# A decoder layer on one core: bias tables by a diagonal product and a slanted store, the memory's keys and values made inside the first block

## The reference, cut to what matters

```python
def t5_bucket(rel):
    n = jnp.maximum(-rel, 0)
    max_exact = N_BUCKETS // 2
    large = max_exact + (jnp.log(jnp.maximum(n, 1).astype(jnp.float32) / max_exact)
                         / math.log(MAX_DIST / max_exact) * (N_BUCKETS - max_exact)).astype(jnp.int32)
    large = jnp.minimum(large, N_BUCKETS - 1)
    return jnp.where(n < max_exact, n, large)

# in causal_block_attention, for each block of 128 queries
rel = positions[:, None, :] - sl(positions)[:, :, None]
bias = jnp.moveaxis(rel_bias[t5_bucket(rel)], -1, 1).astype(jnp.float32)
s2 = jnp.einsum('bqhcd,bkhcd->bhcqk', sl(q_d), k_d).astype(jnp.float32) * diff_scale + bias[:, :, None]
p2 = jax.nn.softmax(jnp.where(mask, s2, NEG), axis=-1)

# in memory_cross_attention; mem_n is the normed memory, 256 rows
q = (h @ w_cq).reshape(b, s, CROSS_HEADS, CROSS_DH)
k, v = jnp.split(mem_n @ w_ckv, 2, axis=-1)
```

## Time and profile before

| | |
|---|---|
| time, median of 3 runs | 4218.0 us (4199.03 to 4221.75) |
| profiled execution, span from first to last instruction | 4102.6 us |
| median less that span (the profiled execution's own whole time is not listed) | 115.4 us |
| busy share: PE, DVE, POOL, ACT | 75%, 62%, 58%, 20% |
| mean DMA rate over the span | 325 GB/s |

### The profile page before, as it was taken

One profiled execution on the slowest core, in us unless ns is written; L12 is line 12 of the kernel. 1 busy time (PEld: TensorE's weight loads), 2 busy tenths in 40 slices (PEclk: granted clock), 3 DMA queues, 4 the chain that ended last, 5 costly groups with the idle time before them and its releaser, 6 DMA issues.

```text
span 4102.6 us, 44198 instructions
## 1 busy us (share of the span) xinstructions
PE 3080.9 (75%) x11072; PEld 1743.0 (42%) x11072; DVE 2523.6 (62%) x6096; ACT 819.6 (20%) x1925; POOL 2390.4 (58%) x2145
## 2 busy tenths in 40 slices
PE   6563789768895789768896788858897589866666
PEld 4442535434452535434452544425454354532222
DVE  8626574766649474766649465585647656476444
ACT  1110231113211231113211132112311123111111
POOL 8100576656756476556766466555565556567776
PEclk9666899879998899879998889979899799988988
DMA  4433999999998999998998899989899888998998
GB/s 142 149 98 128 350 338 399 351 327 335 390 403 308 348 330 396 357 332 325 369 394 307 334 330 376 363 315 333 307 383 343 313 321 308 401 320 318 362 366 327
DMA packets 424948, 1333.13 MB, mean 325 GB/s; under 512 B 47520, under 2 KB 48416, under 8 KB 424672
## 3 DMA queue, kind: packets, MB, share of 16 engines
q0 software_dynamic: 294912, 1073.87, 70.8%
q1 hardware_dynamic: 128608, 251.96, 17.1%
q10 hardware_dynamic: 1152, 4.19, 0.3%
HBM read 1320.46 MB, written 9.37 MB: 324 GB/s over the span
## 4 chain that ended last, share of the span: by engine, by line
PE 47%; DVE 27%; DMA 11%; issue 10%; ACT 3%; POOL 1%; DVEq 0%; POOLq 0%; ACTq 0%; SPq 0%
PE ps_sum L958 22%; PE ps_p L739 9%; PE ps_s L880 6%; DMA rows<-in_peer_v,ids_v 6%; DMA w_ring<-in_wstream 4%; DVE rows L1614 4%; DVE feat_b L1517 3%; DVE feat_b L1512 2%; PE ps_s L823 2%; PE ps_p L831 2%; DVE rows L1306 1%; DVE e L1519 1%; PE ps_s L819 1%; PE ps_t L730 1%; DVE e L1556 1%
## 5 line engine op out<-in xcount | busy, mean ns | idle before, releaser
L958 PE MATMUL ps_sum<-rows,diag 128*128 128x512 f32 x3584 | 1840.4, 650 | 517.9 <-ACT diag L1174 395.7
L546 POOL DMA_INDIRECT rows<-in_peer_u,ids_u x1024 | 1129.4, 1103 | 1171.1 <-DVE dots L1614 562.2
L555 POOL DMA_INDIRECT rows<-in_peer_v,ids_v x1024 | 1167.1, 1140 | 503.6 <-issue 281.3
L1614 DVE CUSTOM_DVE_ANT_0 rows<-rows,h_cur 128x1024 f32<-128x1024 f32 x1024 | 1223.9, 1221 | 200.7 <-DMA rows<-in_peer_u,ids_u 191.3
L958 PEld LDWEIGHTS ps_sum<-rows,diag 128*128 128x128 f32 x3584 | 699.8, 208 | 1388.0 <-issue 984.7
L739 PE MATMUL ps_p<-hT,w_ring 128*128 128x128 f32 x3968 | 520.1, 290 | 78.0 <-DVE hT L1335 56.4
L739 PEld LDWEIGHTS ps_p<-hT,w_ring 128*128 128x128 f32 x3968 | 507.2, 205 | 161.7 <-issue 78.3
L1174 ACT ACTIVATE diag<-ident,acts 128x128 f32<-128x128 f32 x896 | 316.6, 392 | 780.6 <-DVE acts L1637 399.6
L1629 DVE SCALAR_TENSOR_TENSOR x_cur<-rows,acts,x_cur 128x1024 f32<-128x1024 f32 x128 | 164.5, 1285 | 138.1 <-DMA rows<-in_peer_v,ids_v 138.1
L730 PE MATMUL ps_t<-ident,xs 128*128 128x128 f32 x192 | 42.2, 392 | 232.9 <-DVE xs L1323 175.8
L1422 DVE CUSTOM_DVE_ANT_0 e<-ps_s,bias_t 128x512 f32<-128x512 f32 (+3 forms) x96 | 82.2, 857 | 213.6 <-PE ps_s L819 102.7
(11 more groups left out here) (265 smaller groups left out, 2551.7 us busy)
## 6 DMA issues: line engine op xcount, KB each, us to landing
w_ring<-in_wstream SPq DMA_DIRECT2D x816, 256.0 KB, 7.4
bias_t<-bias_rows SPq DMA_DIRECT2D x40, 512.0 KB, 6.5
rows<-in_peer_u,ids_u POOLq DMA_INDIRECT x1024, 6.7
rows<-in_peer_v,ids_v POOLq DMA_INDIRECT x1024, 6.8
bias_rows<-rows SPq DMA_DIRECT2D x5, 960.0 KB, 4.0
bias_t<-in_x SPq DMA_DIRECT2D x8, 512.0 KB, 9.0
out<-x_cur ACTq DMA_DIRECT2D x8, 512.0 KB, 2.8
e<-in_final_gain SPq DMA_DIRECT2D x7, 512.0 KB, 7.4
```

Of the source, the lines that this page charges most:

```text
L546: pool.indirect_dma_start(u_rows[:, j % G_RING, :], None, peer_u, bass.IndirectOffsetOnAxis(ap=ids_u[:, j:j + 1], axis=0)).then_inc(u_land ...
L555: pool.indirect_dma_start(v_rows[:, j % G_RING, :], None, peer_v, bass.IndirectOffsetOnAxis(ap=ids_v[:, j:j + 1], axis=0)).then_inc(v_land ...
L958: ins = pe.matmul(ps_sum[:, c * 512:(c + 1) * 512], diag[:, n % 4, :], v_rows[:, j % G_RING, c * 512:(c + 1) * 512], start=(n == 0), stop= ...
L1614: dve.tensor_tensor_reduce(row, row, h_cur[:, :], 1.0, 0.0, ALU.mult, ALU.add, dots[:, p:p + 1]).then_inc(u_used, 1)
```

## The change

Nothing in blocks 1 to 7 is changed. In the prologue and block 0:

1. **Bias tables.** Partition p stands for the distance 127 - p. DVE compares it with 33 limits in one instruction, takes differences to get the bucket, multiplies the table with it and reduces, which gives the bias at that distance for each head, and puts it on a diagonal. PE multiplies ones by the four diagonals (128 x 128 each), which gives in each partition the same curve of 128 values. ACT copies the curves to SBUF, with the last bucket's value repeated over 896 columns ahead. POOL fills the other 1024 columns with the mask value. A band is now 128 equal rows of 2048 columns; the store gives it its slant, as the rows go to DRAM at a pitch that is one element longer than that of the loads. All five (1 MB each) are issued in a row, without a wait between them, at the start of `project_2`.
2. **Memory.** Its norm and transposes move into `project_0` and `latents` of block 0, and its 32 slices come after the 34 projection slices. PE takes one at each of the positions 24 to 55 of block 0, which lie between `gates` and `diff_3`; ACT's copies have positions too.
3. **x first.** x and the first 7 projection slices are loaded first, and DVE's `scale_x` is the first thing of size that it does.
4. The rotary arguments are made on 128 partitions with 256 columns, and stored with 8 DMAs in place of 2. The decay constants come after `latents`.

```diff
+IN_SLICES = 2 * IN_TILES
+CURVE = 2 * SEQ
+PITCH = CURVE + P
+MEM_AT = 24
...
+        bias_rows = bias_d.rearrange("h (r c) -> h r c", c=PITCH)
+        slanted = bias_d[:, 1:1 + P * (PITCH + 1)].rearrange("h (p c) -> h p c", c=PITCH + 1)
...
# SP
             sp.dma_start(cols[:, :], columns).then_inc(cols_in, 16)
+            sp.dma_start(x_in[:, :], x[0:P, :]).then_inc(x_landed, 16)
...
+            for i in range(W_RING):
+                load_w(MEM_SLICES + i, i)
             for t in range(MT):
-                sp.dma_start((e0, e1)[t][:, :], mem[t * P:(t + 1) * P, :]).then_inc(mem_in, 16)
...
+                sp.dma_start(mem_x[t][:, :], mem[t * P:(t + 1) * P, :]).then_inc(mem_in, 16)
...
+            def store_curves():
+                sp.wait_ge(pre["blank"], DIFF_H + 2)
+                sp.wait_ge(pre["curve"], DIFF_H)
+                for h in range(DIFF_H, -1, -1):
+                    sp.dma_start(slanted[h, :, 0:CURVE], curve[h]).then_inc(pre["stored"], 16)
...
+            def project_2(b):
+                if isinstance(b, int):
+                    store_curves()
+                front_loads(b, per_tile * 7, per_tile * 11)
...
+            def opening(p):
+                i = p - MEM_AT + W_RING
+                if W_RING <= i < MEM_SLICES:
+                    load_w(i, IN_SLICES + i)
+                elif MEM_SLICES <= i < MEM_SLICES + W_RING:
+                    front_loads(0, IN_SLICES + (i - MEM_SLICES), IN_SLICES + (i - MEM_SLICES) + 1)
...
# PE
+            def curves():
+                pe.wait_ge(pre["on_diag"], DIFF_H)
+                for h in range(DIFF_H):
+                    ins = pe.matmul(ps_s[:, h * P:(h + 1) * P], ones[:, :], on_diag[:, h, :], start=True, stop=True)
+                ins.then_inc(pre["curve_ps"], 1)
+
+            def turn_mem():
+                for t in range(MT):
+                    pe.wait_ge(pre["xs"], t + 1)
                     if t:
+                        pe.wait_ge(pre["curve"], DIFF_H)
+                    for k in range(KT):
+                        ins = pe.transpose((ps_sum, ps_s)[t][:, k * P:(k + 1) * P], mem_x[t][:, k * P:(k + 1) * P], ident[:, :])
                     ins.then_inc(pre["turned"], 1)
...
+            def opening(p):
+                if MEM_AT <= p < MEM_AT + MEM_SLICES:
+                    mem_piece(p - MEM_AT)
...
+            def first_project():
+                project(0, 0, 0, 3)
+                curves()
+                turn_mem()
...
# ACT
+            def out_curves():
+                act.wait_ge(pre["curve_ps"], 1)
+                for h in range(DIFF_H):
+                    copy(curve[h][:, 0:near], bc(ps_s[:, h * P:h * P + 1], [P, near]))
+                    copy(curve[h][:, near:SEQ], ps_s[:, h * P:(h + 1) * P]).then_inc(pre["curve"], 1)
...
+            def first_exps():
+                early_exps()
+                project_4(0)
...
# DVE
+                prepare(dve.tensor_scalar(reached, limits, away, None, ALU.is_le))
+                prepare(dve.tensor_tensor(inside, reached[:, 0:BUCKETS], reached[:, 1:BUCKETS + 1], ALU.subtract))
+                prepare(dve.tensor_tensor(picked.rearrange("p (k h) -> p k h", h=DIFF_H), table.rearrange("p (k h) -> p k h", h=DIFF_H),
+                                          bc(inside.unsqueeze(2), [P, BUCKETS, DIFF_H]), ALU.mult))
+                prepare(dve.tensor_reduce(by_away, picked.rearrange("p (k h) -> p h k", h=DIFF_H), AX_X, ALU.add))
+                for h in range(DIFF_H):
+                    dve.tensor_scalar(on_diag[:, h, :], ident[:, :], by_away[:, h:h + 1], None, ALU.mult).then_inc(pre["on_diag"], 1)
...
+            def first_latents():
+                buckets()
+                scale_mem()
+                positions_read()
+                gain_mem()
+                lambdas()
+                latents(0)
+                decays()
```

More of the change, by code:

```diff
@@ L415, in store_mask @@
                             sp.wait_ge(pre["band"], b * (DIFF_H + 1) + (h + 1))
[L416 to L433, removed]
+                            sp.dma_start(bias_rows[h, bass.ds(b * P + P, P), 0:SEQ], rows[:, h, :]).then_inc(pre["stored"], 16)
+                    sp.wait_ge(pre["stored"], 16 * (NB + 1) * (DIFF_H + 1))
                 sp.nop()
@@ new lines, in spread_angles, with rope_sines @@
+            def spread_angles():
+                act.wait_ge(cols_in, 16)
+                at, own = slice(COL["freq"], COL["freq"] + 2), slice(NOPE, NOPE + ROPE)
+                for a in (0, 1, 3):
+                    copy(cols[a * ROPE:(a + 1) * ROPE, at], cols[own, at]).then_inc(pre["spread"], 1)
+            def rope_sines():
+                for c, t in enumerate((cosines, sines)):
+                    act.wait_ge(pre["rope_arg"], c + 1)
+                    act.activation(t, t, ACT.Sin).then_inc(act_step, 1)
+                    act.wait_ge(act_step, c + 1)
+                    if c == 0:
+                        act.nop().then_inc(pre["rope_done"], 1)
+                    else:
+                        act.activation(t, t, ACT.Copy, scale=col("sign")).then_inc(pre["rope_done"], 1)
@@ L1250, in _ @@
-            run(dve.tensor_scalar(rows[:, 11, 0:SEQ - 1], rows[:, 11, 0:SEQ - 1], 1.0, None, ALU.not_equal))
-            run(dve.tensor_reduce(small[:, 5:6], rows[:, 11, 0:SEQ - 1], AX_X, ALU.max))
-            run(dve.tensor_copy(flag[:, :], small[:, 5:6]))
-            dve.nop().then_inc(pre["flag"], 1)
-            r = slice(NOPE, NOPE + ROPE)
-            angle, turns = rows[r, 11, :], e0[r, :]
-            run(dve.tensor_scalar(angle, pos_k[r, :], cols[r, COL["freq"]:COL["freq"] + 1], None, ALU.mult))
@@ new lines, in scale_mem @@
+            def scale_mem():
+                for t in range(MT):
+                    dve.wait_ge(pre["square"], t + 1)
+                    prepare(dve.tensor_scalar(small[:, 124:125], small[:, 122 + t:123 + t], 1.0 / D, EPS, ALU.mult, ALU.add))
+                    rsqrt(small[:, 125:126], small[:, 124:125], small[:, 126:127], prepare)
+                    dve.tensor_scalar(mem_x[t][:, :], mem_x[t][:, :], small[:, 125:126], None, ALU.mult).then_inc(pre["xs"], 1)
+                    dve.wait_ge(pre["xs"], t + 1)
@@ L1669, in _ @@
             hand_over(0)
[L1670 removed]
+            first_steps = steps.n
             finish_steps = 12
```

471 lines of the change are left out of this document (234 added, 237 removed).

## The result

The kernel after took 4142.7 us (median of 4 runs, 4132.6 to 4149.5), the kernel before 4208.5 (4 runs, 4190.9 to 4221.8; three of them are those of the table before the change): a ratio of 0.9852, interval 0.9825 to 0.9878, faster by 65.8 us. Forecast were 4146 us, within 4115 to 4185. A second, later comparison gave 4041.2 us (5 runs) against 4101.2 (9 runs), ratio 0.9855 [0.9837, 0.9872], 60.0 us less. The direction and the size of the gain came out as forecast; that the absolute time did so too is partly luck. Two terms inside were wrong: the head of the kernel gained 10.8 us less than the sum said, and of the 115.4 us that the prediction put "around the profiled span" only some 2 exist.

What follows compares the result with a forecast made beforehand. It took the chain behind block 0 as unchanged, so only block 0's finish, delayed by PE and DVE work, could move. 95.7 + 1.3 - 24.6 = 72.4 us less; 4218 - 72 = 4146 us, range 4115 to 4185.

Steps and rivals of the forecast that it cites:

- around the profiled span: Whole kernel before: 115.4 us taken to lie outside the profiled 4102.6 us span, giving 4218 as the starting time.
- The gain is given back later: Rival: loops of blocks 1 to 7 meet DMA at another phase, or the general way runs; 4218 us, chance 0.04.
- the prediction's own last sign: Behind the first gather: a change of more than 10 us from 3724.7 would show the prediction wrong.
- Step 1: Start of block 0: x first, memory and biases out of the way, hT at 13.5 against 122.9, 109.4 us gained.
- Step 2: Project_0, curves and transposes up to project_1's start at 27.9: 8.4 us added, bounds 5 and 12.
- Step 3: Projection slices: slice 14 queues behind five curve stores at full rate, PE stands 8.7 us, 1.5 more at half clock.
- slow-destination rival: Curve stores: rows starting 4 bytes off a boundary run slowly; at a tenth of the rate 4258 us, chance 0.05.
- no-queue rival: Projections: slices do not queue behind the stores and transposes come earlier; 4131 us, chance 0.18.
- Step 4: Latents to project_4: project_4 done at 69.9 against 165.6, so 95.7 us gained up to there.
- Step 5: Gates and recur: ACT's exponential table load moves away, 1.3 us gained; memory pieces 0 to 5 cost 0.
- Step 6: Block 0's attention: 26 memory pieces between its products make it 65 us against 40.4, 24.6 lost.
- the clock stays low: Rival, block 0's attention: products don't hide, pieces cost twice, 4193 us; partly so, 4170; chance 0.11 together.

Runs made afterwards that it cites:

- base_again: The kernel before, unchanged, profiled once more: 4100.99 us, first gather at 378.3.
- after_again: The changed kernel, unchanged, run again beside the kernel before: 4041.2 us, ratio 0.9855, first gather at 314.4.
- pool_waits: The changed kernel with POOL starting its fills only after DVE has x: first gather at 311.2 us against 314.4.
- quiet: The changed kernel with POOL filling only conv_in, h_last and v_diff and ACT the rest: first gather at 307.6 us against 314.4.
- late_store: The changed kernel with the five curve stores issued in project_4, behind the first 7 memory slices: first gather at 305.5 us against 314.4.
- thin_keys: The changed kernel with one product of four per memory key slice (keys wrong): attention stage 54.1 us against 65.5.

## Why the prediction was right, and where it was not

- **Where the gain is: right.** Everything behind the join moved as a block, 138.9 us to the first gather, and the loops took the same (3719.5 and 3720.8). "The gain is given back later" fell. By the prediction's own last sign it would be wrong, as the part behind the first gather changed by 89.5 us from the profile before (3724.7) to the profile after (3814.2); the pair `base_again` and `after_again`, 1.3 us apart, shows that this is not the change. The sign was no good one, as it set one execution against one.
- **Step 1, x first: wrong by 10 us.** hT came at 23.5, not 13.5. I took the time of the memory's norm in before and did not look at what POOL does beside it. The step failed on "the same operations": DVE's small operations of the gates now stand ahead of x and in the middle of POOL's fills. `pool_waits` and `quiet` show the cause; both put hT at 12, 1.3 us ahead of the forecast.
- **Step 2: right in size** (14.4; 15.1 and 13.4), and what ends it is the one predicted, the wait for the curves on ACT (3.33). Its two parts were off by luck in opposite ways: `project_0` took 7.2 to 8.1 us in place of 6.0, the rest 6.2 to 7.0 in place of 8.4.
- **Step 3, the stores: right.** 8.7 predicted, 9.95 and 10.29 measured, full rate. `project_1` itself took 9.28 at a clock of 0.77 (its window) in place of 8. The slow-destination rival fell by the rates, the no-queue rival by `late_store`. I added 1.5 us for half clock behind the stall: `project_2` took 9.95 and 9.0 us against 7.3 in full clock. I had not seen that the place was a choice: `late_store` gets all of it back.
- **Step 4: right.** 25.3; 25.1 and 24.9. The waits for weights in `project_4` were 2.8 and 2.3 us in place of 2.1 (0.8 as before and 1.3 more); `project_3` at full clock, 7.31 in place of the 8.33 of before, made up for it.
- **Step 5: right** within 2 us, and by `thin_keys` the pieces there cost nothing.
- **Step 6, attention: right,** 65 against 64.7 and 65.5, at clock 0.97, and right in its parts: 60.2 us of work and 5 of waits forecast, 60.8 and 4.6 measured. The rival "the clock stays low" fell.
- **The sum.** 72.4 forecast; 61.6 by the anchors (377.9 to 316.3), 65.8 and 60.0 by the timed comparisons. Of the 10.8 us missing in the anchors step 1 is 10.0; step 3 came out 2.5 long and step 5 1.9 short. The absolute time met the measurement within 3.3 us by luck: a fourth run of before (4190.9) put its median at 4208.5, 9.5 us under the 4218 from which I started, while the timed gain was 6.2 us under the 72 of the forecast. Had the level of the second comparison been met, 4041.2 us would have been far outside the range with the same gain.
- **"Around the profiled span lie 115.4 us": wrong.** About 2 us do (4132.56 and 4130.5; 4100.99 and 4099.1). The profiled execution of before took an estimated 4105 by that, with loops 89.5 us shorter than the profiled one of after (3724.7 and 3814.2 behind the first gather). Its 115.4 us were a difference between executions. The sum survived, as only a difference was carried over.

Left open: why loops with the same instructions run at 345 GB/s in some executions and at 337 in others; no run here tells the chip from anything else. Open too is what lets a held operation in between two fills, as in `pool_waits`, and keeps it out to the end of the row, as in the profile after.

## What to carry to other kernels

Before work is moved to the front, look at what the other engines do there. An operation that was free behind POOL's fills cost 11 us in their midst, and an instruction that takes many times the duration of its like elsewhere is to be read as held, not as work. Bulk stores on the queue of a weight ring did best behind the last slice that is wanted soon; earlier among the slices brought nothing, split up among them a third. Matmul work placed into an attention's gaps was paid at about half its own time (24 to 25 us for 46.7), as it filled PE's idle time and the small products around it ran at the higher clock.

## What the runs showed of the hardware

- DVE held by POOL's memsets: TENSOR_SCALAR of 128x8 for 14.51 us in place of 0.17, through twelve memsets in a row; four of 128x128 8.04 us in place of 0.88, ending 1.8 us ahead of the last fill. TENSOR_TENSOR, a reduction and one-column TENSOR_SCALARs were not held. ACT's fills of the same buffers held no DVE operation.
- Stores of 8 KB rows that start 4 bytes further in each row ran at 393 to 475 GB/s.
- One kernel's median was 4208.5 and 4101.2 us in two comparisons. Of the 96.6 us between two profiled executions of the kernel after, 94.7 lie behind the first gather.
- PE's work in block 0's attention: 26.1 us busy at a granted clock of 0.50, an estimated 14.1 at 0.97 with other products between.
